# Dilated attention by pairs of heads, and the unit behind each norm split ahead of its scales

## The reference

```
def hybrid_mixer(h, w_in, conv_w, g_attn_out, g_conv_out, w_out):
    q, k, v, bg, cg, xc = jnp.split(h @ w_in, 6, axis=-1)        # 512 columns each; 8 heads of 64
    for window, dilation in ((128, 1), (512, 4), (2048, 16)):
        o, lse = dilated_window_attention(q, k, v, window, dilation)   # softmax(q k / 8) v on a causal band
        ...
    mix_w = softmax(stack(lses)); attn = sum(mix_w * outs)
    conv = bg * causal_depthwise_conv3(cg * xc, conv_w)
    merged = concat([rms_norm(attn, g_attn_out), rms_norm(conv, g_conv_out)])
    return merged @ w_out

x = x + hybrid_mixer(rms_norm(x, g_mix), ...)
x = x + memory_cross_attention(rms_norm(x, g_xattn), rms_norm(mem, g_mem), ...)
x = x + squared_relu_mlp(rms_norm(x, g_mlp), w_up, w_down)
```

## Time and profile before

| what | value |
|---|---|
| median of 3 runs | 869.10 us (869.09 to 869.14) |
| profiled execution, its own time | 870.91 us |
| its span, first to last instruction | 869.1 us |
| TensorE busy | 856.0 us (98%) |
| VectorE busy | 541.8 us (62%) |
| ScalarE busy | 394.6 us (45%) |
| mean granted clock of TensorE | 0.995 |

### The profile page before, as it was taken

The page is one execution under the profiler, slowest core; times in us unless marked ns, Lnnn a source line. Parts: engine busy times, 40 slices in busy tenths (PEclk is TensorE's granted clock), DMA queues, the critical chain, the costliest instruction groups (busy, mean ns, idle before and its releaser), DMA issues.

```text
span 869.1 us, 16493 instructions
## 1 busy us (share of the span) xinstructions
PE 856.0 (98%) x7230; PEld 790.6 (91%) x7230; DVE 541.8 (62%) x595; ACT 394.6 (45%) x464; POOL 6.8 (1%) x8
## 2 busy tenths in 40 slices
PE   9999999999999999999999999999999999999997
PEld 9999899998989999999999989988898899999996
DVE  5998754535777665555557655477654666655564
ACT  7552331356267544343447344456534544444332
POOL 0000110000000000000000000000000000000000
PEclk9999999999999999999999999999999999999999
DMA  9845412121474756555652744426353465555541
GB/s 296 281 140 193 146 51 99 51 98 51 167 253 137 243 158 219 173 176 192 194 193 98 242 146 146 146 98 225 130 179 97 130 209 193 184 177 185 187 140 49
DMA packets 96747, 140.62 MB, mean 162 GB/s; under 512 B 2480, under 2 KB 79408, under 8 KB 96688
## 3 DMA queue, kind: packets, MB, share of 16 engines
q1 hardware_dynamic: 96400, 139.62, 48.6%
q10 hardware_dynamic: 288, 0.13, 0.1%
HBM read 138.69 MB, written 1.05 MB: 161 GB/s over the span
## 4 chain that ended last, share of the span: by engine, by line
PE 93%; DVE 3%; ACT 2%; issue 1%; POOL 1%; POOLq 0%; DVEq 0%; ACTq 0%
PE PS L414 91%; ACT xh L1139 1%; DVE wlo L1553 1%; PE PS L519 1%; ACT whi L1139 1%; DVE xl L1584 0%; PE PS L974 0%; PE PS L643 0%; POOLq L97 0%; DVE xn L2099 0%; POOL TT L1128 0%; POOL TT L1132 0%; ACT junk L1139 0%; PE PS L1053 0%; DVE XT L1704 0%
## 5 line engine op out<-in xcount | busy, mean ns | idle before, releaser
L1553 DVE TENSOR_TENSOR wlo<-raw,whi 128x2048 fp32r<-128x2048 f32 x124 | 283.4, 2290 | 152.0 <-ACT whi L1139 151.9
L414 PE MATMUL PS<-xh,whi 128*128 128x256 f32 x1136 | 324.1, 287 | 3.3 <-DVE wlo L1553 2.0
L414 PE MATMUL PS<-xh,wlo 128*128 128x256 f32 x1136 | 320.7, 284 | 0.0
L414 PE MATMUL PS<-xl,whi 128*128 128x256 f32 x1136 | 317.0, 284 | 0.0
L1139 ACT ACTIVATE whi<-raw 128x2048 fp32r<-128x2048 f32 (+1 forms) x130 | 241.0, 1857 | 162.7 <-PE PS L414 162.4
L414 PEld LDWEIGHTS PS<-xh,whi 128*128 128x128 f32 x1136 | 218.4, 192 | 9.6 <-issue 3.5
L414 PEld LDWEIGHTS PS<-xh,wlo 128*128 128x128 f32 x1136 | 218.5, 192 | 0.0
L414 PEld LDWEIGHTS PS<-xl,whi 128*128 128x128 f32 x1136 | 216.2, 192 | 1.0
L414 PE MATMUL PS<-whi,fh 128*128 128x512 f32 x216 | 84.3, 391 | 0.0
L414 PE MATMUL PS<-wlo,fh 128*128 128x512 f32 x216 | 84.3, 390 | 0.0
L414 PE MATMUL PS<-whi,fl 128*128 128x512 f32 x216 | 84.0, 389 | 0.0
(11 more groups left out here) (305 smaller groups left out, 1086.2 us busy)
## 6 DMA issues: line engine op xcount, KB each, us to landing
raw<-in_w_in_dram SPq DMA_DIRECT2D x32, 1024.0 KB, 5.3
raw<-in_w_up_dram SPq DMA_DIRECT2D x16, 1024.0 KB, 5.3
raw<-in_w_down_dram SPq DMA_DIRECT2D x16, 1024.0 KB, 5.0
raw<-in_w_ffn_gate_dram SPq DMA_DIRECT2D x11, 1024.0 KB, 5.5
raw<-in_w_ffn_up_dram SPq DMA_DIRECT2D x11, 1024.0 KB, 5.3
raw<-in_w_ffn_down_dram SPq DMA_DIRECT2D x11, 1024.0 KB, 5.0
raw<-in_w_kv_mem_dram SPq DMA_DIRECT2D x8, 1024.0 KB, 5.4
raw<-in_w_o_dram SPq DMA_DIRECT2D x4, 1024.0 KB, 8.2
```

The costliest lines, as they stand in the source:

```text
L414: return nc.tensor.matmul(o, l, r, start=start, stop=stop, **kw)
L1553: V.tensor_tensor(wlo[u % RING][:], raw[u % RING][:], whi[u % RING][:].bitcast(f32), ALU.subtract) \
```

## The change

Two things change.

*Behind the norms.* At n2 and n3 ScalarE rounds the second unit right behind the eight roundings of the residual, ahead of the second square, the root and the keys' copy; VectorE subtracts it ahead of `inverse`. At n4 and n5 VectorE subtracts two quarters of that unit between the residual's additions (`lo_piece`), and the rest behind `inverse`.

*Dilated attention.* Heads are taken over by pairs: the even head lies on the lower 64 partitions of q2 and k2, the odd one on the upper 64, and their matmuls stand next to each other. dz, dp and dq are one buffer each, for both heads. The logits of a pair go to banks 4 and 5, those of the first pair between the two value units. The four exponentials are followed by a reciprocal of their sums and four scalings of dp on VectorE (semaphore d_w), for which the six transposes wait. The values are now the stationary operand (64 columns per head) and the turned weights the moving one (256 and 128 columns), so the output comes with features on partitions, normalised, in banks 6 and 7. `att`, `transpose_scaled`, `deviation` and `diagonal` go; the attention's norm is made like the convolution's: square (an), `sum_rows`, root (ars), reciprocal, four scalings, rounding, subtraction. A head pair is laid over two fill units: logits, fill, turn, fill, values.

The diff, cut to its core:

```diff
@@ TensorE
-            for i, u in enumerate(U_V2):
-                by_token(u, xh, xl, 4 * i, 2, i == 0, i == 1)
...
-            def head_out(h):
-                pe.wait_ge(sem("d_q"), h + 1)
-                hs = slice(h * HD, (h + 1) * HD)
-                mm(bank(6)[:, hs], dq[h % 2][:, 0:P], v2[:, 0, hs], True, True)
-                mm(bank(7)[:, hs], dq[h % 2][:, P:SEQ], v2[:, 0, hs], True, False)
-                mm(bank(7)[:, hs], dq[h % 2][:, SEQ:384], v2[:, 1, hs], False, True).then_inc(sem("d_o"), 1)
...
+            by_token(U_V2[0], xh, xl, 0, 2, True, False)
+
+            def dilated_logits(p_):
+                if p_ == 0:
+                    pe.wait_ge(sem("out2_evac"), 4)
+                else:
+                    pe.wait_ge(sem("d_z_read"), p_)
+                for e in range(2):
+                    mm(PS[:, (4 + e) * 512:(4 + e) * 512 + P], q2[half(e), p_, 0:P], k2[half(e), p_, 0:P], True, True)
+                for e in range(2):
+                    last = mm(PS[:, (4 + e) * 512 + P:(4 + e) * 512 + 384], q2[half(e), p_, P:SEQ], k2[half(e), p_, :], True, True)
+                last.then_inc(sem("d_z"), 1)
+
+            def dilated_turn(p_):
+                pe.wait_ge(sem("d_w"), p_ + 1)
+                if p_ == 0:
+                    pe.wait_ge(sem("v2_ready"), 2)
+                for e in range(2):
+                    for c in range(3):
+                        o = (2 + e) * 512 + c * P
+                        last = nc.tensor.transpose(PS[:, o:o + P], dp[:, e, c * P:(c + 1) * P], C("ident"))
+                last.then_inc(sem("d_T"), 1)
+
+            def dilated_values(p_):
+                pe.wait_ge(sem("d_q"), p_ + 1)
+                o = (6 + p_ // 2) * 512 + p_ % 2 * SEQ
+                for e in range(2):
+                    mm(PS[half(e), o:o + SEQ], v2[:, 0, head(2 * p_ + e)], dq[:, e, 0:SEQ], True, False, skip_group_check=True)
+                for e in range(2):
+                    last = mm(PS[half(e), o + P:o + SEQ], v2[:, 1, head(2 * p_ + e)], dq[:, e, SEQ:384], False, True, skip_group_check=True)
+                last.then_inc(sem("d_o"), 1)
...
+            dilated_logits(0)
+            by_token(U_V2[1], xh, xl, 4, 2, False, True)
+            for p_ in range(NPAIR):
+                if p_:
+                    dilated_logits(p_)
+                dilated_fill(2 * p_)
+                dilated_turn(p_)
+                dilated_fill(2 * p_ + 1)
+                dilated_values(p_)
...
@@ ScalarE
                 round_T(st, g, xh, 0, range(KD), place, last_of)
+                if filler:
+                    hi(U_KM[filler - 1] - 1 + RING)
                 act.wait_ge(norm_sem(st, "x"), nth(st, "x", 4))
...
+            dilated_exp(0)
             after(U_V2[1])
...
+            for p_ in range(NPAIR):
+                if p_:
+                    hi(FILL2[2 * p_ - 1] + RING)
+                    act.wait_ge(sem("d_T"), p_)
+                    dilated_exp(p_)
+                hi(FILL2[2 * p_] + RING)
+                act.wait_ge(sem("d_T"), p_ + 1)
+                if p_:
+                    act.wait_ge(sem("d_o"), p_)
+                A_(dq[:], PS[:, 2 * 512:4 * 512].rearrange("p (e n) -> p e n", e=2)[:, :, 0:384], ACT.Copy).then_inc(sem("d_q"), 1)
...
@@ VectorE
+            def lo_piece(u, a, b):
+                if a == 0:
+                    dve.wait_ge(sem("hi_done"), u + 1)
+                r = slice(a, b)
+                last = V.tensor_tensor(wlo[u % RING][:, r], raw[u % RING][:, r], whi[u % RING][:, r].bitcast(f32), ALU.subtract)
+                if b == UNIT:
+                    last.then_inc(sem("unit_split"), 1)
...
+                        if then != "fin" and (t, c) in ((0, 1), (1, 0)):
+                            lo_piece(u - 1 + RING, 512 * t, 512 * t + 512)
...
-                inverse(st)
-                if u not in (U_F["d", FF_CHUNKS - 1], U_O[3]):
-                    lo(u - 1 + RING)
-                lo(u + RING)
                 if u == U_O[3]:
+                    lo(u + RING)
+                    inverse(st)
                     lo(U_KM[0] + RING)
...
+            dilated_max(0)
+            lo(U_V2[1] + RING)
+            for p_ in range(NPAIR):
+                if p_:
+                    dilated_max(p_)
+                    lo(FILL2[2 * p_ - 1] + RING)
+                dve.wait_ge(sem("d_p"), p_ + 1)
+                link(V.reciprocal(col(DRL + 4 * p_, 4), col(DL + 4 * p_, 4)))
+                for t, r in enumerate((slice(0, P), slice(P, 384))):
+                    for e in range(2):
+                        last = V.tensor_scalar(dp[:, e, r], dp[:, e, r], col(DRL + 4 * p_ + 2 * t + e), None, ALU.mult)
+                last.then_inc(sem("d_w"), 1)
+                fill_evac(2 * p_)
+                lo(FILL2[2 * p_] + RING)
+                fill_evac(2 * p_ + 1)
```

More of the change, by code:

```diff
@@ L234, in block_kernel @@
         for n in ("T", "hi", "xT"):
-            EVENTS[n] = {n: NPAIR if n == "att" else KD for n in TURNED}
+            EVENTS[n] = {n: KD for n in TURNED}
         def norm_sem(st, what):
@@ L1159, in after @@
                 act.wait_ge(sem("units_used"), u + 1)
-            def deviation(st, src, ready, width=D):
-                c = NORM[st]
-                for t in range(NT):
-                    ready(t)
-                    A_(junk[:, 0:width], src(t), ACT.Square, accum_out=col(c + t)).then_inc(norm_sem(st, "sq"), 1)
-                    act.wait_ge(norm_sem(st, "sq"), nth(st, "sq", t + 1))
-                    A_(col(c + 2 + t), col(c + t), ACT.Sqrt, scale=1.0 / width, bias=col(EPS)).then_inc(norm_sem(st, "sd"), 1)
             def part_ready(base, u, t, c):
@@ L1460, in _ @@
             values_evac(0)
-            for j in range(NPAIR):
-                act.wait_ge(sem("conv_n"), j + 1)
-                A_(m2h[:, 4 + j, :], cv[:, 0, j, :], ACT.Copy).then_inc(sem("conv_hi"), 1)
+            half_round(1, cv[:, 0])
             values_evac(1)
```

191 lines of the change are left out of this document (74 added, 117 removed).

## The result

The changed kernel takes 864.11 us (median of 4 runs, 863.82 to 864.22), the kernel before 869.12 on the same chip: a ratio of 0.9931, 95% interval 0.9918 to 0.9943. Forecast were 863.6 us, 861.0 to 866.4. The profiled execution of the changed kernel took 864.22 us, its span is 862.4 against 869.1, so 6.7 us less, where the medians differ by 5.0. These two have two each.

The account below looks back on a forecast made before the run. TensorE, busy 856.0 of 869.1 us, was taken to bound the kernel. 869.1 - 1.85 (norms) - 5.3 (blocks) + 1.65 (new wait), tail 0, gave 863.6 us, range 861.0 to 866.4.

Parts of the forecast that it names:

- Part 1, norms: Unit behind each norm n2 to n5: TensorE's waits for VectorE's low part shrink or go, 1.85 us saved (1.0 to 2.1).
- n4 and n5: At these norms only half the low part stays behind the diagonals; TensorE's 0.42 us wait goes, 0.45 us saved each.
- Part 2, blocks: TensorE's small blocks in the dilated attention: removed 15.15 us, added 9.85 us for pairs, 5.3 us saved (4.5 to 6.0).
- Part 3, the new wait: First turn: transposes wait for weights VectorE scales only after a low part queued ahead, 1.65 us lost (1.0 to 2.2).
- The cover at the other turns: In the three later pairs, scaled weights are ready 0.3 us before TensorE wants them, so 0 wait (0 to 0.5 each).
- A chance of 0.22 for a wait of 1.65: Rival at the first turn: the clock falls to half for 3.4 us, 1.7 us more, 865.3 us; chance 0.22.
- Part 4, tail: Behind the dilated attention, to the output projection: VectorE's changed work costs TensorE 0 us (0 to 0.5).
- The wait isn't there: Rival at the first turn: a step of the chain is shorter than added up, no wait, 862.0 us; chance 0.11.
- each turn is late: Rival at the three later turns: the cover is gone, 0.3 to 1 us lost at each, 865.5 us; chance 0.12.
- the norms give nothing: Rival at the norms: the scale matmuls' wait eats the split's gain, 1.85 us lost, 865.4 us; chance 0.05.
- slower: Rival at all four turns: every pair waits behind a low part and the clock falls at each, 875.4 us; chance 0.03.
- The halves don't overlap: Rival in the pairs' values and logits: two heads' matmuls don't run together, 6.6 us more, 870.2 us; chance 0.03.

Follow-up runs that it names:

- norms-alone run: The kernel before with only the change behind the norms n2 to n5, heads one by one as before: 866.14 us, ratio 0.9952.
- the kernel with the scaling first: The changed kernel with VectorE's reciprocal and four scalings of the first pair's weights moved ahead of the low part that stood before them: 860.74 us, ratio 0.9893.
- the longer waits: The changed kernel with 512, 1024 or 2048 columns subtracted again ahead of that low part (864.36, 864.77, 868.71 us), or first logits behind the second value unit (866.73 us).
- the kernel with the pairs alone: The changed kernel with the norms as in the kernel before, so only the dilated attention's change stays: 864.66 us, ratio 0.9934.

## Why the prediction was right, point by point

The sign, the size and the place of every part were right; the forecast lies 0.5 us from the median. Span against span it was too careful by 1.2 us (5.5 forecast, 6.7 measured), and the carrying over to the median took back most of that: by its time, the profiled execution of before had one half-clock stretch more than those of which its median (869.10) is made, while the changed kernel's four runs all lie near the 864.22 of its profiled one, which had two. So 863.6 is close partly by luck, because a gain sized too small and a clock that I did not count cancel.

- *Part 1, norms.* Forecast 1.85 us, measured 2.47. n3 (0.79 for 0.7) and n2 (0.34 for 0.25) are right, with the new wait of 0.15 in front of the scale matmuls measured as 0.16. The mis-sized terms are n4 and n5: 0.45 forecast, 0.66 and 0.68 measured. I took the printed idle of 0.42 for what can be won. The end of a matmul's record is modelled and lies behind the time at which its successor could start; the gap has to be read from start to start, 1.03 before and 0.37 after. I had that rule for the blocks and didn't use it for the waits. The norms-alone run agrees.
- *Part 2, blocks.* Forecast 5.3, measured 5.96 from start to start (98.45 before, 92.49 in the kernel with the scaling first, where no wait stands). Logits 0.86 (0.85). The values are 0.80 for three pairs and 0.85 for the last, so most of the entry of 0.1 that I added to each isn't there (0.35 in all). Six transposes cost 0.57 to 0.58 and not 0.66 (0.35), and the two 0.1 for a break between the value units and for a wait of the first memory-value unit don't show. A fill unit behind a turn takes 5.92 instead of 5.86 (0.24 back). The sum of squares (1.54) and the transposition that went (1.70) cancelled to 0.16; on the removed side the values were 5.42 in place of 5.7 and the transposes 2.78 in place of 2.65. The base, two heads for the price of one from the earlier trace rows, was the right row, now with proof (1.29 us a pair when they share a half). The Trainium skill, page "TensorEngine Tiling (Array Packing)", "Key Properties", says that different tiles can load weights and multiply in parallel; these runs agree. Its Gotcha 1, on one PSUM bank, speaks of row tiles only; the values are column tiles, and both heads' in one bank took 0.80 us, 1.44 when they shared a half.
- *Part 3, the new wait.* The mechanism and its place were right. I had added it up from start to start, 1.65 us, and so measured it is 1.42 at the turn (1.26 printed). From the first low part to the turn, which starts 0.05 behind the end of the scaling, the chain takes 11.42 us (502.61 to 514.03), forecast 11.63; from there to the time at which TensorE wants the turn it is 10.01 (to 512.62, which is 17.75 behind the first value unit as in the kernel without the wait), forecast 9.98. So the chain was some 0.2 too long in my sum and TensorE's side was right. No single step is off by more than 0.15 us; mostly the records' durations that I added are longer than the distance from start to start, as for the low part (2.29 and 2.21). The cover at the other turns was forecast as 0.3 us and is 0.4 (scaling done at 527.7, turn at 528.09). That the clock doesn't fall was right for 1.26 us. It would have been wrong for a wait of 1.99; where between the two it turns, and so whether it would have held at my own 1.65, no run tells. A chance of 0.22 for a wait of 1.65 was too low given what the longer waits did, and the trace of before held a nearer row than the wait of 0.81 that I set against it:

```profile
216.70 1.15 PE L414 MATMUL PS<-grs,cst 8*128 8x128 f32 x8 [1.18 <-DVE grs L1799]
```

  Behind this wait and eight narrow matmuls the clock stood at 0.50 for 3.4 us from 217.90. I also put the price of a fallen clock at 1.7 us; a stretch of 3.4 us cost 1.5.
- *Part 4, tail.* 0 forecast; the rows behind the last fill unit show no wait.
- *Rivals.* "The wait isn't there", "each turn is late", "the norms give nothing" and "slower" did not come. "The halves don't overlap" was tested: it would have cost 5.2 us, forecast 6.6.

## What to carry to other kernels

A wait for an engine that the trace shows idle at that time is an order in a queue: look at what stands ahead of the awaited instruction, whether that can move behind it, and then list every semaphore for which the waiting instruction asks, since the second one may be hidden behind the first. Read gains from start to start on TensorE, not from the printed idle time, and look at the granted clock of the stretches of both executions before two spans are subtracted. Before lengthening a short wait on TensorE, allow for the clock: here 0.7 us more of waiting cost 2.2, in one execution.

## What the runs showed of the chip

**The clock falls after short waits.** In this place it held for waits of 1.10 us (one execution) and 1.26 (four) and fell for 1.99, 2.52, 3.32 and 3.59, one execution each. The price was 1.5 us for a stretch of 3.4 us and 2.5 to 2.6 for one of 6.8. The whole shows it: span 862.6 for the wait of 1.99, against 860.4 for the changed kernel (each with a stretch at 63 us besides), so 2.2 us for 0.73 us of waiting.

**It also falls at two places ahead, in some executions and not in others.** Windows of the changed kernel's profiled execution (span 862.4), and of the same kernel run again (860.4, with one timeline row of TensorE between them), clock behind the busy times:

```profile
65.05:68.46 3.41, 3.41 (x19) 3.41 (x18) 3.41 (x5) 0.00 (x0) 0.00 (x0) 0.50 0.85 280
218.65:222.06 3.41, 3.41 (x18) 3.41 (x17) 1.20 (x2) 0.63 (x1) 0.00 (x0) 0.50 0.49 131
```

```profile
63.52:66.94 3.42, 3.42 (x19) 3.42 (x18) 3.42 (x7) 0.00 (x0) 0.00 (x0) 0.50 0.57 166
216.49 1.15 PE L415 MATMUL PS<-grs,cst 8*128 8x128 f32 x8 [1.17 <-DVE grs L1791]
217.00:222.00 5.00, 4.99 (x41) 4.33 (x41) 2.62 (x3) 0.99 (x2) 0.00 (x0) 1.00 0.43 136
```

The first place follows the eight matmuls on 8 rows, and TensorE isn't idle there. The second follows eight of 128 columns on 8 rows, and ahead of these a wait of 1.17 to 1.18 us for the row grs in every execution. So a wait of this length was followed by a fall in ten of the thirteen profiled executions, and in three it was not; the narrow matmuls behind it are what the first turn of the attention doesn't have.

Each stretch costs 1.5 us. Across the first place, from TensorE's start behind a wait for wlo near 9 us to its start behind a wait for TT near 112 us, it is 102.9 us with the stretch and 101.4 without (101.75 in the kernel with the pairs alone). Across the second, from the grs matmuls to the scale matmuls of n2, it is 64.6 us with it in the changed kernel and 63.1 without. The times of a kernel lie in steps that fit 0, 1 or 2 of them, and the mean granted clock of the executions agrees: before 867.66 (0.999), 869.0 to 869.3 (0.996 to 0.997), 870.7 to 871.2 (0.994 to 0.995); the changed kernel 862.1 to 862.3 (0.996 to 0.997) and 863.5 to 864.2 (0.994 to 0.995). Of the thirteen profiled executions five had both stretches, five the second alone and three the first alone. Nothing in the edits goes with it: the same kernel showed one and two.

One thing in the traces does go with it: when the clock rose at the start. The first stretch, where there is one, begins 58.03 us after that rise, the second 211.63 after it, and the one at the attention's first turn 508.6 after it, in every trace. Where the clock rose at 4.05 to 4.82 us only the second stretch came, at 5.24 to 5.50 only the first, and at 5.57 to 7.03 both. This is an order among thirteen executions and not an experiment: no run sets the rise, and none removes the narrow matmuls. If it is a cause, whether a short wait brings a fall depends also on when it comes after that rise, and the waits above, one execution for each length that fell, give no safe length. Why the rise comes when it does stays open.
